# Experts' order: two weight tiles of the next expert split ahead, outputs scattered behind the first two tiles

## The reference, cut to what matters

```python
for e in range(N_EXPERTS):          # 8
    y = y + combine[..., e:e + 1] * swiglu(h, wg[e], wu[e], wd[e])
# swiglu(h, wg, wu, wd) = (silu(h @ wg) * (h @ wu)) @ wd,  hidden width 1408
x = x + mod_x[5] * y
```

## Time and profile before

| | |
|---|---|
| median of 3 runs | 1634.97 us (1633.97 to 1642.86) |
| the profiled execution's own time | 1644.77 us, span 1643.0 us |
| mean granted TensorE clock | 0.950 |
| busy over the span | PE 1461.8, DVE 960.7, ACT 589.6 us |
| expert loop, first gate_up to the last gather | 1113.7 to 1607.7 us |

### The profile page before, as it was taken

One profiled execution on the slowest core, in us unless ns is written; L12 is line 12 of the kernel. 1 busy time (PEld: TensorE's weight loads), 2 busy tenths in 40 slices (PEclk: granted clock), 3 DMA queues, 4 the chain that ended last, 5 costly groups with the idle time before them and its releaser, 6 DMA issues.

```text
span 1643.0 us, 20249 instructions
## 1 busy us (share of the span) xinstructions
PE 1461.8 (89%) x7622; PEld 1159.5 (71%) x7622; DVE 960.7 (58%) x1349; ACT 589.6 (36%) x982; POOL 343.2 (21%) x272
## 2 busy tenths in 40 slices
PE   5799999789979999999979995868998998898895
PEld 2587877455468888888859983666777777777774
DVE  2844424766374444343477646538777777777783
ACT  2311133363121110010041143526656656656562
POOL 0109999900010000000014997000000000000000
PEclk9799999889989999999989998979999999999997
DMA  9145532452212222222213310058776867867800
GB/s 370 73 154 217 219 154 103 165 195 103 88 66 93 87 103 103 97 96 97 109 51 129 106 50 0 1 218 335 291 287 249 306 256 279 307 250 276 317 1 26
DMA packets 30017, 263.92 MB, mean 161 GB/s; under 512 B 3328, under 2 KB 3328, under 8 KB 4224
## 3 DMA queue, kind: packets, MB, share of 16 engines
q1 hardware_dynamic: 29952, 263.01, 42.5%
HBM read 261.95 MB, written 1.05 MB: 160 GB/s over the span
## 4 chain that ended last, share of the span: by engine, by line
PE 75%; DVE 9%; POOL 8%; ACT 4%; issue 3%; DMA 1%; ACTq 0%; DVEq 0%; SPq 0%
PE ps L456 33%; PE ps L816 16%; PE ps L836 6%; POOL sb_arena L1764 4%; PE ps L702 4%; POOL sb_arena L1767 3%; PE ps L469 3%; PE ps L786 2%; PE ps L795 2%; PE ps L486 1%; DVE sb_rows_n L1468 1%; DVE sb_egu_lo L1622 1%; PE ps L588 1%; PE ps L635 1%; ACT sb_ew_hi L1141 1%
## 5 line engine op out<-in xcount | busy, mean ns | idle before, releaser
L456 PE MATMUL ps<-sb_h_hi,sb_w_hi 128*128 128x512 f32 (+1 forms) x640 | 242.4, 379 | 9.8 <-DVE sb_h_lo L1286 9.8
L456 PE MATMUL ps<-sb_h_lo,sb_w_hi 128*128 128x512 f32 (+1 forms) x640 | 241.5, 377 | 0.0
L456 PE MATMUL ps<-sb_h_hi,sb_w_lo 128*128 128x512 f32 (+1 forms) x640 | 240.9, 376 | 0.0
L1285 DVE CAST sb_w_hi<-sb_arena 128x2048 fp32r<-128x2048 f32 (+1 forms) x58 | 74.3, 1281 | 214.9 <-PE ps L456 141.7
L1764 POOL TENSOR_SCALAR sb_arena<-sb_arena,sb_small 128x512 f32<-128x512 f32 (+1 forms) x120 | 176.7, 1473 | 11.8
L816 PE MATMUL ps<-sb_egu_lo,sb_h_lo 128*128 128x512 f32 (+1 forms) x384 | 147.7, 385 | 0.0
L456 PEld LDWEIGHTS ps<-sb_h_hi,sb_w_hi 128*128 128x128 f32 x640 | 122.2, 191 | 32.4 <-DVE sb_h_lo L1286 10.6
L1767 POOL TENSOR_TENSOR sb_arena<-sb_arena 128x512 f32<-128x512 f32 (+1 forms) x120 | 138.3, 1152 | 10.0
L456 PEld LDWEIGHTS ps<-sb_h_hi,sb_w_lo 128*128 128x128 f32 x640 | 122.2, 191 | 21.8
L456 PEld LDWEIGHTS ps<-sb_h_lo,sb_w_hi 128*128 128x128 f32 x640 | 122.2, 191 | 21.6
L1286 DVE TENSOR_TENSOR sb_w_lo<-sb_arena,sb_w_hi 128x2048 fp32r<-128x2048 f32 (+1 forms) x58 | 134.2, 2314 | 2.0
(11 more groups left out here) (286 smaller groups left out, 2857.0 us busy)
## 6 DMA issues: line engine op xcount, KB each, us to landing
sb_arena<-experts SPq DMA_DIRECT2D x88, 1536.0 KB, 8.4
sb_arena<-mod SPq DMA_DIRECT2D x48, 1024.0 KB, 5.1
sb_arena<-in SPq DMA_DIRECT2D x24, 1024.0 KB, 4.8
sb_arena<-gate SPq DMA_DIRECT2D x11, 1024.0 KB, 4.8
sb_arena<-up SPq DMA_DIRECT2D x11, 1024.0 KB, 4.8
sb_arena<-out SPq DMA_DIRECT2D x8, 1024.0 KB, 4.8
sb_arena<-down SPq DMA_DIRECT2D x8, 1024.0 KB, 4.8
sb_arena<-down SPq DMA_DIRECT2D x4, 768.0 KB, 4.1
```

The source lines that it names most:

```text
L456: ins = pe.matmul(o, left[a], right[b], start=(k == first and n == 0), stop=(k == final and n == len(PRODUCTS) - 1))
L1285: settled(v.tensor_copy(hi, x), ("hi", key))
```

## The change

ACT and DVE split tiles 0 and 1 (AHEAD = 2) of the next expert at the end of the present round, and once before the loop for the first expert: tile 0 between the parts of tiles 9 and 10 for down, tile 1 as the last thing of the round. `take_output` comes right at a round's start on ACT, with leading(0) and leading(1) behind it. On PE quarters 0 and 1 are scattered behind gate_up(0), quarters 2 and 3 behind gate_up(1), and the transposes of the shares move from tile 6 to tile 8. On DVE the shares come first, add_output(0, 1) behind gate_up_rest(2), quarter 2 at tile 5, quarter 3 at tile 6, and the tables at tile 9. Because the last round too splits two tiles ahead, SP loads tiles 0 and 1 of expert 0 once more at the end; the loop then splits them, and nobody uses them.

```diff
+            for f in range(AHEAD):
+                sp.wait_ge(down_done, n * ET + (f + 1))
+                sp.dma_start(experts[:, f, :], A["experts"][0, f]).then_inc(sem_exp[f], 16)
@@ PE
-                        if f == 3:
+                        if f == 0:
                             pe.wait_ge(y_act, i + 1)
                             pe.wait_ge(from_slot_ready, i + 1)
                             scatter(i, (0, 1))
-                        if f == 5:
+                        if f == 1:
                             scatter(i, (2, 3))
-                        if f == 6:
+                        if f == 8:
                             pe.wait_ge(shares_built, i + 1)
@@ ACT
                     f(spare, eps, ACT.Silu)
-                    for t in range(ET):
-                        gate_up_leading(t)
-                        if t == 1:
-                            act.wait_ge(down_done, i * ET + ET)
-                            act.wait_ge(scattered, i * 4 + 4)
-                            take_output()
-                        if t >= 3:
+                    act.wait_ge(down_done, i * ET + ET)
+                    act.wait_ge(scattered, i * 4 + 4)
+                    take_output()
+                    leading(0)
+                    leading(1)
+                    for t in range(AHEAD, ET):
+                        gate_up_leading(i, t)
+                        if t >= 5:
                             leading(t - 3)
+                        if t == ET - 1:
+                            leading(ET - 3)
...
                     hidden_leading(PAIRS - 2)
-                    leading(ET - 3)
                     silu(PAIRS - 1)
                     leading(ET - 2)
+                    gate_up_leading(i + 1, 0)
+                    leading(ET - 1)
                     take_input(i + 2)
                     hidden_leading(PAIRS - 1)
-                    leading(ET - 1)
+                    gate_up_leading(i + 1, 1)
@@ DVE
+                    dve.wait_ge(shares_turned, i + 1)
...
+                    for t in range(AHEAD, ET):
+                        gate_up_rest(i, t)
+                        if t == 2:
+                            add_output(i, (0, 1))
                         if t >= 3:
                             rest(t - 3)
...
                         if t == 5:
-                            add_output(i, (2, 3))
-                        if t == 8:
+                            add_output(i, (2,))
+                        if t == 6:
+                            add_output(i, (3,))
+                        if t == 9:
                             dve.wait_ge(shares_turned, i + 2)
...
+                    rest(ET - 3)
                     hidden_rest(PAIRS - 2)
-                    rest(ET - 3)
                     hidden_product(PAIRS - 1)
                     rest(ET - 2)
+                    gate_up_rest(i + 1, 0)
+                    rest(ET - 1)
                     take_input(i + 2)
                     hidden_rest(PAIRS - 1)
-                    rest(ET - 1)
+                    gate_up_rest(i + 1, 1)
```

More of the change, by code:

```diff
@@ L43 @@
 HALF = KD * P
+AHEAD = 2
 EPS = 1e-6
@@ L1127, in take_output, with gate_up_leading, leading @@
                     ins.then_inc(y_act, 1)
-                take_input(1)
+                def gate_up_leading(i, t):
+                    act.wait_ge(sem_exp[t], i * 16 + 16)
+                    for a in range(2):
+                        x = 2 * t + a
+                        act.wait_ge(gu_used, i * 2 * ET + (half_before(x) + 1))
+                        f(glead[x % 4], experts[:, t, a * HALF:(a + 1) * HALF].rearrange("p (a n) -> p a n", a=4), ACT.Copy)\
+                            .then_inc(gu_leading, 1)
+                take_input(1)
+                for t in range(AHEAD):
+                    act.wait_ge(sem_exp[t], 16)
+                    for a in range(2):
+                        f(glead[2 * t + a], experts[:, t, a * HALF:(a + 1) * HALF].rearrange("p (a n) -> p a n", a=4), ACT.Copy)\
+                            .then_inc(gu_leading, 1)
                 with act.Fori(0, n) as i:
-                    def gate_up_leading(t):
+                    def leading(t):
                         act.wait_ge(sem_exp[t], i * 16 + 16)
[L1133 to L1139, removed]
                         act.wait_ge(down_done, i * ET + (down_before(t) + 1))
@@ L1155, in moe @@
                     f(spare, eps, ACT.Silu)
-                    for t in range(ET):
-                        gate_up_leading(t)
-                        if t == 1:
-                            act.wait_ge(down_done, i * ET + ET)
-                            act.wait_ge(scattered, i * 4 + 4)
-                            take_output()
-                        if t >= 3:
+                    act.wait_ge(down_done, i * ET + ET)
[6 more added lines that the diff above has]
+                        if t >= 5:
                             leading(t - 3)
-                        if t >= 2 and t % 2 == 0:
+                        if t == ET - 1:
+                            leading(ET - 3)
+                        if t % 2 == 0:
                             silu(t // 2 - 1)
-                        if t >= 3 and t % 2:
+                        else:
                             hidden_leading((t - 3) // 2)
                     hidden_leading(PAIRS - 2)
-                    leading(ET - 3)
                     silu(PAIRS - 1)
                     leading(ET - 2)
+                    gate_up_leading(i + 1, 0)
+                    leading(ET - 1)
                     take_input(i + 2)
                     hidden_leading(PAIRS - 1)
-                    leading(ET - 1)
+                    gate_up_leading(i + 1, 1)
                 act.wait_ge(down_done, n * ET + ET)
@@ L1613, in add_output, with gate_up_rest @@
                         ins.then_inc(x_added, 1)
+                def gate_up_rest(i, t):
+                    for a in range(2):
+                        x = 2 * t + a
+                        dve.wait_ge(gu_leading, i * 2 * ET + (x + 1))
+                        v.tensor_tensor(egu_lo[t][:, a * HALF:(a + 1) * HALF].rearrange("p (a n) -> p a n", a=4),
+                                        experts[:, t, a * HALF:(a + 1) * HALF].rearrange("p (a n) -> p a n", a=4),
+                                        glead[x % 4].bitcast(F32), ALU.subtract).then_inc(gu_split, 1)
                 build_slots(0, 1)
                 take_input(1)
+                for t in range(AHEAD):
+                    gate_up_rest(0, t)
                 with dve.Fori(0, n) as i:
[L1618 to L1624, removed]
                     def rest(t):
@@ L1641, in hidden_rest @@
                                         ALU.subtract).then_inc(glu_done, 1)
[L1643 to L1652, removed]
+                    dve.wait_ge(shares_turned, i + 1)
+                    for b in range(2):
+                        ins = v.tensor_scalar(shares[:, b, :], slots, column(slot_no, i, b), column(share, i, b),
+                                              ALU.is_equal, ALU.mult)
+                    ins.then_inc(shares_built, 1)
+                    for t in range(AHEAD, ET):
+                        gate_up_rest(i, t)
+                        if t == 2:
+                            add_output(i, (0, 1))
                         if t >= 3:
                             rest(t - 3)
-                        if t >= 2 and t % 2 == 0:
+                        if t % 2 == 0:
                             hidden_product(t // 2 - 1)
-                        if t == 4:
-                            add_output(i, (0, 1))
+                        else:
+                            hidden_rest((t - 3) // 2)
                         if t == 5:
-                            add_output(i, (2, 3))
-                        if t == 8:
+                            add_output(i, (2,))
+                        if t == 6:
+                            add_output(i, (3,))
+                        if t == 9:
                             dve.wait_ge(shares_turned, i + 2)
```

## The result

| | before | after |
|---|---|---|
| median | 1636.34 us (1633.97 to 1642.86, 4 runs) | 1578.4 us (1575.14 to 1579.15, 4 runs) |
| ratio | | 0.9636, 95% interval 0.9604 to 0.9668 |
| profiled execution, span | 1643.0 us | 1576.0 us |
| granted clock over the span | 0.950 | 0.968 |
| gather to gather, mean of 7 | 62.97 us | 55.75 us |

The kernel is 58 us faster. The median before is that of four runs; the forecast started from 1634.97, that of the first three. Lines have moved: gate_up is L820 (was L816), down L840 (L836), gather L790, scatter L799, the gate_up rests L1633 (L1622), hidden_rest L1656 (L1640), take_input L1125 and L1615, add_output L1625.

The account below looks back on a forecast made before the run. PE's idle time in the expert loop is what can be won: 46.7 us in seven periods, 4.0, 1.0 and 1.1 sum to 52.8, so 1592 profiled; as median 1586, between 1582 and 1595; range 1568 to 1608.

Parts of the forecast that it names:

- The waits that go: PE in the expert loop: waits before down(8) of 1.30, gate_up(0) of 0.80 and gate_up(6) of 2.10 us disappear.
- The wait before down(10): PE near the gather: 0.9 us stays of 2.05, now behind hidden_rest(5); bounds 0.5 and 2.05.
- The new wait at the scatter: PE before scatter quarter 2: about 1.0 us for add_output(0), queued behind gate_up_rest(2); bounds 0.3 and 2.1.
- PE's own work: PE's time per period without waits: 54.4 us, taken between 53.8 and 55.0.
- The clock in the loop: PE's clock in the expert loop: 1.00, since no wait of 2 us or more is left.
- The sum: Whole kernel: 52.8 us saved, 46.7 of it in seven periods, giving 1592 for the profiled execution.
- The first expert: First expert up to its gather: loses 2.1, 1.3 and a slow stretch of 1.6, gets 1.0; saves 4.0 us.
- The rival in which short idle times are enough for the clock to go to and fro: PE's clock in the loop still falls at the two waits left: 1600 to 1605 us; chance 0.15.
- The end: After the last gather: the last down(10) saves 1.1 us.
- From the profiled execution to the median: The median lies 9.8 us under the profiled execution: 1582 if the gain is whole, 1595 otherwise; 1586 taken.
- The loads: Weight loads capped at 275 GB/s: period stays 63, 1635 us, chance 0.03; most gain kept, 1610 to 1625, 0.04.
- The slower rival: ACT at the next expert's tile 0 waits for a late load, holding up PE: up to 1653 us; chance 0.03.

Follow-up runs that it names:

- experiment 1: Changed kernel with scatter, add_output, shares and tables back at their old tiles, two tiles still split ahead: 1597.12 us, ratio to before 0.9750.
- experiment 2: Kernel before with only scatter, add_output, shares and tables at their new places, nothing split ahead: 1620.62 us, ratio 0.9896.
- experiment 4: Changed kernel with add_output(0, 1) on DVE before gate_up_rest(2) instead of behind it: 1572.63 us.
- experiment 6: Changed kernel with add_output(0, 1) before gate_up_rest(2) and the last pair's turn before the gather: 1570.76 us, ratio to before 0.9584.
- experiment 3: Changed kernel with AHEAD = 1, tile 1 split behind leading(0) at the round's start: 1587.15 us, ratio to before 0.9708.
- experiment 9: Kernel before, unchanged, run again for a second profile: 1638.02 us, profiled span 1631.7 us.
- experiment 8: Changed kernel with the loads of the next expert's tiles 0 to 6 held back until after down(6): 1587.93 us.
- experiment 5: Changed kernel with the last pair's turn before the gather on PE, its hidden_leading and hidden_rest before take_input: 1580.26 us.
- experiment 10: Changed kernel, unchanged, run again on the same chip as its variants: 1580.62 us.

## Why the prediction was right

The forecast was 1586 with a range of 1568 to 1608; the time is 1578.4. Step by step:

- **The waits that go.** Those before down(8), gate_up(0) and gate_up(6) are gone, and experiments 1 and 2 bring back the last, or the first two with the old wait before down(10), by undoing one part.
- **The wait before down(10).** Laid out as 0.9 of 2.05, behind hidden_rest; 0.86 and this releaser in the trace. The orders of events on ACT and DVE fit to 0.2 us, and so do the durations.
- **The new wait at the scatter.** Laid out as 1.0, it is 0.54. The place and the queue behind it were right, the term was about twice too high (taking the wait away, in experiment 4, gave 0.83).
- **PE's own work.** Between 53.8 and 55.0 I took the middle, 54.4, with no reason for just that value; here I was lucky. The period of 55.75 less 0.86 and 0.54 is 54.35, and experiment 6, without waits, runs at 54.24.
- **The clock in the loop.** No fall in any of the seven periods, and in experiment 6 neither. The nine falls that the seven periods before had were worth 12.0 us, so the 50.5 us won there are some 38.5 of waits and 12.0 of clock. The rival in which short idle times are enough for the clock to go to and fro is not borne out. The Trainium skill ("TensorE: Matmul & The Clock Gate", A second HAM failure mode: psum-queue depth-cycling) tells of a kernel whose clock went to and fro because PE stood idle briefly, but frequently, between groups of matmuls. This case does not show it: two idle times of 0.86 and 0.54 us in each period of 56 us never brought a fall, nor did those of 0.86 and 1.75 in experiment 3, while waits of about 2 us did sometimes.
- **The sum.** The seven periods gave 50.5 for 46.7, since both waits together are 0.5 shorter. The first expert gave 2.7 for 4.0, because the slow stretch of 1.6 that I counted as gone is there in both profiles: the clock is at 1.2 GHz for a time behind the wait before the first gate_up, before (0.57 over 1113.5 to 1117.5) and after (0.57 over 1106.5 to 1110.5), and 4.0 less 1.6 is 2.4. The start of the loop (the tile ahead of the table load) gave 1.6 for 1.0, once the 6.8 us of the low stretch ahead are taken off. The end was under-sized: 1.1 was forecast and 5.4 came. I had counted the wait before the last down(10) alone (1.2 of it); in the profile before, the clock fell behind it, and the last down (0.8), the scatter (5.78 us, now 4.09) and the sum of squares (5.41, now 3.72) ran slow, as the rows under this list show. In experiment 9 the scatter is slow too (5.85), but the sum of squares is not (3.72), so its 1.7 us are chance. The profiled execution came 14 us under the 1592 worked out for it, and 8.5 of them, these 1.7 and the 6.8, are chance.
- **From the profiled execution to the median.** I left open whether the 9.8 us between them lay in the loop or elsewhere. Experiment 9 settles it for that second execution: its loop has falls as the first had, and 9.7 us of its 11.3 are ahead of the loop. The whole gain counts; the forecast by that reading was 1582, and my 1586 was a compromise with one that does not hold.
- **The rivals.** The loads are not the bound: at 308 to 318 GB/s nothing waits for them, even when they are held back until down(4). The slower rival's mechanism works (experiment 8), but the median of 8.4 us for a landing overstates what tile 0 needs: it was there some 6.8 us after down(6), 5.6 of my clock and 1.21.

The end of the kernel before and of the changed one, scatter and sum of squares:

```profile
1618.83 5.78 PE L795 MATMUL ps<-sb_rstd,sb_H 128*128 128x256 f32 x16 [1.53 <-ACT sb_H L1126]
1627.70 5.41 PE L890 MATMUL ps<-sb_arena,sb_con 128*128 128x256 f32 x16 [3.10 <-ACT sb_arena L1209]
```

```profile
1555.24 4.09 PE L799 MATMUL ps<-sb_rstd,sb_H 128*128 128x256 f32 x16 [1.54 <-ACT sb_H L1130]
1562.43 3.72 PE L894 MATMUL ps<-sb_arena,sb_con 128*128 128x256 f32 x16 [3.10 <-ACT sb_arena L1223]
```

What I did not see before the runs is that the two waits left have one root, ACT's unbroken run after the gather. Experiment 5 removed the first and got nothing, experiment 4 the second and got 0.8 us a period, and only both together free PE.

## What to carry to other kernels

Where engines work in order, ask of each wait not only who released it but what that engine had standing in front: here splitting two tiles ahead of their round and scattering sooner gave 58 us, and moving sums ahead of subtractions that were not ready, with a turn ahead of a gather, 10 more, with no work taken out of a period. Two waits in a row on the bound engine that go back to the same late queue are one wait: removing the first alone moves it to the second, so start with the second. Lay the new order out on paper with measured durations; it found both leftover waits, their places and their releasers before the kernel had run.

## What the runs showed of the hardware that I had not expected

- The same wait of 2.10 us before a gate_up had the clock fall to 1.2 GHz in six of the seven periods of the kernel before, and in none of the seven of experiment 1. In experiment 2 the clock fell at the waits of the boundary, which the kernel before has too, and cost five periods of seven 2.7 us (61.47 against 58.76, clock 0.94), another 0.5, and one none. In experiment 8 it fell behind waits of 1.91 and 1.92 us before down(10) and not behind one of 2.12. The length of a wait alone does not say whether the clock falls; what does, these runs leave open.
- One and the same code ahead of the loop took up to 9 us more or less from one execution to the next. The kernel before starts its first gather at 1103.32 us with a stretch of PE's clock at half speed (0.83 over 340 to 400 us) and at 1094.61 without it (1.00); the changed kernel and its variants start it at 1103.71 (experiment 5) and at 1094.74 (experiment 10). A difference of two profiles has to be cut at a landmark before its parts are explained.
